# Eight weight copies placed at staggered SBUF addresses, with small statistics tensors in the gaps

## What is computed

```python
mod = (silu(c) @ w_mod + b_mod)[:, None, :]            # shift, scale, gate, twice
h = rms_norm(x, norm1_g) * (1.0 + sc1) + sh1
z = h @ w_in                                           # 2048 -> all heads, gates and conv channels
mixed = concat([fox(z), nsa(z), conv(z)])
x = x + g1 * (mixed @ w_out)                           # 2048 -> 2048
h = rms_norm(x, norm2_g) * (1.0 + sc2) + sh2
x = x + g2 * (square(relu(h @ w_mlp1)) @ w_mlp2)       # 2048 -> 8192 -> 2048
return rms_norm(x, final_g)
```

## Time and profile before

| | |
|---|---|
| runs | 1172.91, 1173.09, 1174.53 us; median 1173.09 us |
| profiled execution | span 1172.2 us from first to last instruction; its own time outside the span isn't recorded apart |
| TensorE busy | 1134.7 us, 97% |
| VectorE busy | 983.7 us, 84% |
| ScalarE busy | 641.5 us, 55% |
| granted TensorE clock | 0.989 of full speed as a mean |
| DMA | 314.65 MB moved, 268 GB/s as a mean |

### The profile page before, as it was taken

The page is one execution under the profiler, slowest core; times in us unless marked ns, Lnnn a source line. Parts: engine busy times, 40 slices in busy tenths (PEclk is TensorE's granted clock), DMA queues, the critical chain, the costliest instruction groups (busy, mean ns, idle before and its releaser), DMA issues.

```text
span 1172.2 us, 17842 instructions
## 1 busy us (share of the span) xinstructions
PE 1134.7 (97%) x7087; PEld 1005.2 (86%) x7087; DVE 983.7 (84%) x1182; ACT 641.5 (55%) x936; POOL 23.6 (2%) x40
## 2 busy tenths in 40 slices
PE   4999999999999999999999999999999999999996
PEld 4899989999887778999788888888888888888885
DVE  5998989988997988997887788987778987878774
ACT  6655458877775546544454445554455544445452
POOL 1000000100000000010000000000000000000000
PEclk6999999999999999999999999999999999999999
DMA  9999998878966897985657675657674667666451
GB/s 372 420 420 420 421 409 310 255 205 281 358 227 249 301 304 292 401 351 183 210 186 266 240 282 180 215 187 277 238 270 176 218 202 263 251 231 262 152 180 72
DMA packets 48322, 314.65 MB, mean 268 GB/s; under 512 B 6572, under 2 KB 8440, under 8 KB 11768
## 3 DMA queue, kind: packets, MB, share of 16 engines
q1 hardware_dynamic: 44592, 305.72, 70.1%
q0 software_dynamic: 1760, 5.26, 2.4%
q10 hardware_dynamic: 1896, 2.64, 0.8%
HBM read 305.20 MB, written 4.21 MB: 264 GB/s over the span
## 4 chain that ended last, share of the span: by engine, by line
PE 76%; DVE 11%; DMA 5%; ACT 4%; issue 3%; SPq 0%; ACTq 0%; DVEq 0%
PE quad L1285 15%; PE quad L1299 10%; PE quad L1300 10%; PE quad L1301 10%; PE quad L1287 8%; PE quad L1275 5%; PE quad L1276 5%; PE quad L1277 5%; DMA first_raw<-in_w_mod 3%; DVE w_lo L1850 3%; PE quad L1346 2%; PE quad L1345 2%; PE quad L1347 2%; DVE mod_raw L1857 2%; DMA mod_raw<-in_w_mod 2%
## 5 line engine op out<-in xcount | busy, mean ns | idle before, releaser
L893 ACT ACTIVATE w_hi<-raw 128x1024 fp32r<-128x1024 f32 (+1 forms) x342 | 355.4, 1044 | 304.9 <-PE quad L1301 115.9
L1850 DVE TENSOR_TENSOR w_lo<-raw,w_hi 128x1024 fp32r<-128x1024 f32 (+1 forms) x342 | 408.3, 1204 | 112.4 <-ACT w_hi L893 110.4
L1285 PE MATMUL quad<-act,w_hi 128*128 128x512 f32 x768 | 266.4, 390 | 0.0
L1275 PE MATMUL quad<-act,w_hi 128*128 128x256 f32 x760 | 215.2, 283 | 6.0 <-DVE w_lo L1850 3.9
L1287 PE MATMUL quad<-act,w_lo 128*128 128x256 f32 x768 | 216.6, 282 | 0.0
L1276 PE MATMUL quad<-act,w_hi 128*128 128x256 f32 x760 | 213.1, 280 | 0.0
L1277 PE MATMUL quad<-act,w_lo 128*128 128x256 f32 x760 | 213.1, 280 | 0.0
L1285 PEld LDWEIGHTS quad<-act,w_hi 128*128 128x128 f32 x768 | 144.2, 188 | 30.2
L1275 PEld LDWEIGHTS quad<-act,w_hi 128*128 128x128 f32 x760 | 144.1, 190 | 8.7 <-issue 4.6
L1299 PE MATMUL quad<-w_hi,u_hi 128*128 128x512 f32 x376 | 148.8, 396 | 0.6 <-DVE u_lo L2307 0.6
L1301 PE MATMUL quad<-w_hi,u_lo 128*128 128x512 f32 x376 | 148.7, 396 | 0.0
(11 more groups left out here) (371 smaller groups left out, 1715.6 us busy)
## 6 DMA issues: line engine op xcount, KB each, us to landing
raw<-in_w_main SPq DMA_DIRECT2D x184, 1024.0 KB, 5.0
mod_raw<-in_w_mod SPq DMA_DIRECT2D x67, 1024.0 KB, 7.2
first_raw<-in_w_mod SPq DMA_DIRECT2D x14, 1024.0 KB, 15.3
late_raw<-in_w_mod SPq DMA_DIRECT2D x10, 1024.0 KB, 7.9
acc<-in_w_mod SPq DMA_DIRECT2D x4, 1024.0 KB, 12.5
conv_b<-conv_q POOLq DMA_DIRECT2D x8, 512.0 KB, 5.2
x_a<-in_x SPq DMA_DIRECT2D x2, 1024.0 KB, 7.2
x_scratch<-x SPq DMA_DIRECT2D x1, 2048.0 KB, 11.7
```

The source lines that it names most:

```text
L893: A(dst[:, 0:2 * width], block_half(raw, j, width), ACT.Copy).then_inc(hi_done, 1)
L1275: mm(out, hi, act_hi[:, k, :], start=begin and m % 2 == 0, stop=False, skip_group_check=True)
L1285: mm(out, w_hi[j % 4][:, cols], act_both[:, k, :, :].rearrange("p h t -> p (h t)"), start=begin, stop=False, skip_group_check=True)
L1850: TTn(lo[:, 0:2 * width], block_half(raw, j, width), hi[:, 0:2 * width].bitcast(f32), ALU.subtract)\
```

## The change

The eight weight copies are no longer allocated one right behind the other. Behind each of them one small tensor is allocated that was further back before: `seen`, `pos_sum`, `mean_sq`, `root`, `rstd`, `part_ms`, `newton`, `ssq_end`. Each of these takes 32 bytes.

```diff
         raw = [sb(f"raw{i}", [P, 4 * GW]) for i in range(4)]
-        w_hi = [sb(f"w_hi{i}", [P, 2 * GW], f32r) for i in range(4)]
-        w_lo = [sb(f"w_lo{i}", [P, 2 * GW], f32r) for i in range(4)]
+        w_hi = [sb("w_hi0", [P, 2 * GW], f32r)]
+        seen = sb("seen", [P, 1])
+        w_hi += [sb("w_hi1", [P, 2 * GW], f32r)]
+        pos_sum = sb("pos_sum", [HD, 2])
+        w_hi += [sb("w_hi2", [P, 2 * GW], f32r)]
+        mean_sq = sb("mean_sq", [P, TT])
+        w_hi += [sb("w_hi3", [P, 2 * GW], f32r)]
+        root = sb("root", [P, TT])
+        w_lo = [sb("w_lo0", [P, 2 * GW], f32r)]
+        rstd = sb("rstd", [P, TT])
+        w_lo += [sb("w_lo1", [P, 2 * GW], f32r)]
+        part_ms = sb("part_ms", [P, TT])
+        w_lo += [sb("w_lo2", [P, 2 * GW], f32r)]
+        newton = sb("newton", [P, TT])
+        w_lo += [sb("w_lo3", [P, 2 * GW], f32r)]
+        ssq_end = sb("ssq_end", [P, TT, 2])
         mod_raw = [sb(f"mod_raw{i}", [P, D]) for i in range(2)]
```

More of the change, by code:

```diff
@@ L272, in build @@
         b_col = sb("b_col", [P, 4 * KT])
-        seen = sb("seen", [P, 1])
         c_col = sb("c_col", [P, KT])
@@ L280, in build @@
         ssq = sb("ssq", [P, 3, TT, 4])
[L281 to L286, removed]
         bf_b = sb("bf_b", [P, NFOX])
@@ L293, in build @@
         pos_t = sb("pos_t", [P, CMP_STRIDE])
-        pos_sum = sb("pos_sum", [HD, 2])
         rel_t = sb("rel_t", [NB, NNSA])
```

## The result

The changed kernel takes 1175.38 us (median of 20 runs, 1174.36 to 1177.24), the kernel before 1173.7 us in the same comparison (20 runs, 1172.29 to 1175.52). The ratio is 1.0014, with a 95% interval of 1.0008 to 1.002: 0.14% slower. That is less than the 0.2% that I had named as the bound for "no change", but it is clear of zero, and it is 7.3 us from my 1168.1.

The account below looks back on a forecast made before the run. TensorE's matmuls were taken to bound the kernel, above all from 545 us on. Only the moving copies counted: 1172.2 - 5.0 = 1167.2 us of span, plus 0.9 us, gave 1168.1 us; range 1162 to 1177 us.

Parts of the forecast that it names:

- no change: Whole kernel: differences below about 0.2%, 2.3 us, can't be told from an unchanged time; "same" had chance 0.33.
- What bounds the kernel: From 545 to 1163 us TensorE is busy 617.41 of 618 us, so its matmuls set the length.
- VectorE, ScalarE and what lies behind, at nothing: Copying operations and DMA destinations: no dependence on address seen, at most 0.3 us on VectorE, nothing reaching the end.
- TensorE, weight copy as moving operand: a dependence is seen: Lines 1299 to 1301: odd halves gain 6.6 ns in each of 756 matmuls, 5.0 us gained.
- my 756 x 6.6 over 1512: Lines 1299 to 1301: 756 of 1512 counted matmuls lie in odd halves and gain 6.6 ns each, 5.0 us.
- TensorE, weight copy as stationary operand: taken as nothing: Lines 1275 to 1277 and up groups: between 2.5 us gain and 3.8 us loss, set to 0.
- both neighbours: Evidence for the stationary bounds: the last group's 0.443 ns a column for the gain, line 1346's 283 against 280 ns for the loss.
- The slower rival: Stationary copies in 1908 odd-half matmuls cost 2 ns each, moving side gains nothing: +3.8 us, 1176.9 us; chance 0.20.
- The sum: Whole kernel: span 1172.2 - 5.0 = 1167.2 us, plus 0.9 us to the median, 1168.1 us, 0.43% faster; chance 0.36.

Follow-up runs that it names:

- the shift by 32: All eight weight copies moved alike by 32 bytes against the kernel before, by allocating only `seen` ahead of them; ratio 1.0018.
- the kernel with the stagger alone: Against the changed kernel: high copies kept, each low copy put at exactly 256 from its high copy modulo 512; ratio 1.0016 against the kernel before.

## Why the prediction was wrong, point by point

**What bounds the kernel: right.** TensorE's matmuls set the length from 545 us on. The change of their intervals came out at the end: +1.66 us in the stages, +1.68 us in the medians.

**VectorE, ScalarE and what lies behind, at nothing: right.** 1221 and 1058 ns after the change, and the kernel that moves only what is behind has 0.9996.

**"TensorE, weight copy as moving operand: a dependence is seen": right as a mechanism, wrong as a rule.** The dependence is there, and its size was nearly right: the shift by 32 runs 5.5 ns below the kernel before, where I had 6.6 from fifteen intervals. But "a moving operand which begins at 32 from a multiple of 64 runs fast" is no rule of the chip. What counts is how far the moving operand lies from the stationary one; with all copies shifted alike, 256 bytes fit as the period: of the eight distances in steps of 32 one gives 227.8 ns, one 229.3, and six 232.7 to 234.0. In the change only `w_hi1` has the first and `w_hi3` the second, and their low copies, 128 bytes off, have neither. That offset takes even more away: in the last quarter most halves with `w_hi1` go at 233.3 ns as before, and those with `w_hi0`, `w_hi2` and `w_hi3` at about 232.1, 232.5 and 230.4. The moving copies gained 233.3 - 232.2 = 1.1 ns over all, where my 756 x 6.6 over 1512 comes to 3.3 ns. Behind 545 us 1.13 of 3.7 us arrived.

**"TensorE, weight copy as stationary operand: taken as nothing": this is the step that failed.** I had the bounds, a gain of 2.5 and a loss of 3.8 us, and set the value to zero because both neighbours seemed weak. It measured +0.75 us in the first up part and +2.04 us in the other three, 2.8 us together. My bound of 3.8 us was for all 3816 matmuls; for the roughly 2300 of them behind 456 us it comes to 2.3 us, so the loss was a little beyond it. The slower rival had the right place (stationary copies) and nearly the right size. Its reason, that operands placed alike cost on the stationary side, is what the shift by 32 shows: 116.7 to 119.9 ns where weight copy and activation are at the same place modulo 256, even a little over the 3 ns I took as its end. But it named the odd halves, and that isn't what the change shows: in the first up part the matmuls with `w_hi0` to `w_hi3` take 118.8, 119.1, 118.0 and 114.9 ns, all 116.7 before. `w_hi0` hasn't moved; the kernel with only the low copies moved has 118.8 too. So what costs `w_hi0` is where the low copies stand, which no term and no rival of the prediction had. It isn't the whole loss: without that offset the kernel with the stagger alone has the same mean, 117.7 ns. The rival's other half, that the moving side gains nothing, was wrong.

**The page of the Trainium skill.** "SBUF — State Buffer", section "Who interferes with whom", has TensorE's two read ports independent and TensorE waiting on no one. By it nothing would have changed. The measurement decides otherwise: with the same instructions the same matmul takes 227.8 or 234.0 ns, by where the operands lie to each other alone. Whether the two reads meet in the memory or somewhere else on the way, no run here shows.

**The sum.** With the measured terms, 1704 x -1.1 + 2280 x 1.0 + 768 x 2.6 ns = -1.9 + 2.3 + 2.0 = +2.4 us, against +1.7 measured; the part of it that lies in the DMA-heavy first stage can be absorbed there. Against the prediction that is 3.1 us less gain from the moving copies and 4.3 us of loss from the stationary ones: the first alone would have left the change faster, the second turned the sign.

## What to carry to other kernels

Where TensorE is full, compare the intervals between starts of matmuls of one shape whose operands lie at different low addresses, and take the pair of moving and stationary operand as the unit, not one of them, together with the operands of the matmuls next to it: parts at mixed distances don't give the mean of their distances. A tensor that is moving in one stage and stationary in another pays on both sides, so shift the partner that appears in one stage only: 32 bytes between `arena` and `hold` gave 0.48% here, while ten placements of the weight copies, the change's among them, cost 0.14% to 0.71%. A stagger "against conflicts" that samples all distances gave about the mean of good and bad ones here, or less; two places in a trace are too few to make a rule of.

## What was not expected of the hardware

- A 512-column matmul with a weight copy moving took 227.8 to 234.0 ns by the distance of its two operands in the low bits of the address, with all copies shifted alike (2.7%), a 256-column one with the copy stationary 115.8 to 119.9 ns (3.5%), a pair of 512 and 256 columns 346.7 to 353.3 ns (1.9%).
- Shifts of 32 and of 288 bytes gave the same intervals to 0.1 ns, and moving the one operand or the other by 32 bytes gave the same to 0.2 ns.
- The effect doesn't need DMA traffic: 226.7 against 232 to 233 ns stood in a stretch with a DMA share of 0.01. VectorE was busy there for 12 of 16 us, and no run has the matmuls without the other engines.
- The place of a low copy changed the interval of the high copy next to it in the stream, by 1.8 ns (116.6 to 118.4), though the high copy had not moved. In the change the same kind of neighbour took the gain from `w_hi1`: 233.3 ns against 228.3.
